# The causal convolution's output turned back to tokens on VectorE, 32x32 blocks at a time

## The reference

```
z = (u @ w_in).astype(float32)
aq, af, ai, ag, bq, bk, bv, bg, ba, bb = split(z, cuts)
o_a = _hgrn2(aq, af, ai, lb)
qkv = silu(_causal_conv(concatenate([bq, bk, bv]), conv_w))    # 4 taps, one filter for each of 3072 channels
bq, bk, bv = split(qkv, [1024, 2048])
q = l2norm(bq as 8 heads of 128) * 128 ** -0.5
k = l2norm(bk as 8 heads of 128)
o_b = _gated_delta(q, k, bv, beta, log_decay)                  # in chunks
o = concatenate([o_a gated, o_b gated])
return o @ w_out
```

## Time and profile before

| | us |
|---|---|
| time, median of 3 runs | 2742.45 |
| lowest and highest | 2741.99, 2743.88 |
| profiled execution | 2741.93 |
| its span (first to last instruction) | 2740.1 |
| PE busy in it | 2714.2 |
| DVE busy | 1684.5 |
| ACT busy | 1344.0 |

### The profile page before, as it was taken

The page is one execution under the profiler, slowest core; times in us unless marked ns, Lnnn a source line. Parts: engine busy times, 40 slices in busy tenths (PEclk is TensorE's granted clock), DMA queues, the critical chain, the costliest instruction groups (busy, mean ns, idle before and its releaser), DMA issues.

```text
span 2740.1 us, 32409 instructions
## 1 busy us (share of the span) xinstructions
PE 2714.2 (99%) x13136; PEld 2261.2 (83%) x13136; DVE 1684.5 (61%) x2280; ACT 1344.0 (49%) x1952; POOL 62.3 (2%) x85
## 2 busy tenths in 40 slices
PE   9999999999999999999999999999999999999998
PEld 7788888888888888888888888888888888887877
DVE  5666665565666666545645555666666664466666
ACT  6645444554444444434544555644444443355565
POOL 0000000000000000000100000000000000000002
PEclk9999999999999999999999999999999999999999
DMA  7764655756666666666665434666666666665444
GB/s 231 135 139 123 116 125 124 205 192 200 193 193 192 193 197 194 192 193 196 205 194 154 123 108 162 195 196 186 199 193 194 194 194 193 193 206 164 161 138 132
DMA packets 213494, 480.61 MB, mean 175 GB/s; under 512 B 15584, under 2 KB 16480, under 8 KB 212704
## 3 DMA queue, kind: packets, MB, share of 16 engines
q1 hardware_dynamic: 210848, 467.32, 59.1%
q0 software_dynamic: 2352, 11.17, 1.2%
q10 hardware_dynamic: 144, 0.05, 0.0%
HBM read 476.38 MB, written 2.10 MB: 175 GB/s over the span
## 4 chain that ended last, share of the span: by engine, by line
PE 90%; DVE 5%; ACT 2%; issue 1%; DMA 1%; POOL 0%; SPq 0%; ACTq 0%; POOLq 0%
PE PS L1116 19%; PE PS L1118 19%; PE PS L1117 19%; PE PS L1163 8%; PE PS L1164 8%; PE PS L1165 8%; DVE WL L2183 1%; DVE WORK L2350 1%; ACT WH L1657 1%; PE PS L1379 1%; PE PS L1263 1%; PE PS L1515 1%; PE PS L1282 1%; PE PS L1091 1%; DVE XL L2183 0%
## 5 line engine op out<-in xcount | busy, mean ns | idle before, releaser
L2183 DVE TENSOR_TENSOR WL<-RAW,WH 128x1024 fp32r<-128x1024 f32 x826 | 1010.5, 1225 | 817.1 <-ACT WH L1657 814.7
L1657 ACT ACTIVATE WH<-RAW 128x1024 fp32r<-128x1024 f32 x830 | 875.3, 1056 | 924.8 <-PE PS L1118 610.7
L1116 PE MATMUL PS<-WH,UTH 128*128 128x512 f32 x2396 | 951.9, 397 | 3.3 <-DVE WL L2183 1.8
L1118 PE MATMUL PS<-WH,UTL 128*128 128x512 f32 x2396 | 934.3, 390 | 0.0
L1117 PE MATMUL PS<-WL,UTH 128*128 128x512 f32 x2396 | 933.7, 390 | 0.0
L1116 PEld LDWEIGHTS PS<-WH,UTH 128*128 128x128 f32 x2396 | 450.4, 188 | 99.3 <-issue 5.2
L1118 PEld LDWEIGHTS PS<-WH,UTL 128*128 128x128 f32 x2396 | 449.9, 188 | 96.1
L1117 PEld LDWEIGHTS PS<-WL,UTH 128*128 128x128 f32 x2396 | 450.7, 188 | 88.3
L1163 PE MATMUL PS<-WH,HTH 128*128 128x512 f32 x656 | 255.2, 389 | 0.0
L1164 PE MATMUL PS<-WL,HTH 128*128 128x512 f32 x656 | 255.2, 389 | 0.0
L1165 PE MATMUL PS<-WH,HTL 128*128 128x512 f32 x656 | 255.2, 389 | 0.0
(11 more groups left out here) (420 smaller groups left out, 2211.7 us busy)
## 6 DMA issues: line engine op xcount, KB each, us to landing
RAW<-in_ffn_w_gu SPq DMA_DIRECT2D x352, 512.0 KB, 4.4
RAW<-in_ffn_w_down SPq DMA_DIRECT2D x176, 512.0 KB, 4.6
RAW<-in_ab_w_in SPq DMA_DIRECT2D x128, 512.0 KB, 4.8
RAW<-in_nsa_w_in SPq DMA_DIRECT2D x80, 512.0 KB, 3.6
RAW<-in_w_in SPq DMA_DIRECT2D x64, 512.0 KB, 4.1
RAW<-in_ab_w_out SPq DMA_DIRECT2D x32, 512.0 KB, 4.2
RAW<-in_nsa_w_out SPq DMA_DIRECT2D x32, 512.0 KB, 4.3
RAW<-in_w_out SPq DMA_DIRECT2D x16, 512.0 KB, 4.4
```

Source lines behind the costliest of these rows:

```text
L1116: e.matmul(o, lh, wh[:, j], start=k + j == 0, stop=False)
L1118: x = e.matmul(o, ll, wh[:, j], start=False, stop=k + j == NKT - 1)
L1657: e.activation(wh, raw, ACTF.Copy).then_inc(*a_hi.inc(s))
L2183: e.tensor_tensor(wl, raw, wh.bitcast(F32), ALU.subtract).then_inc(*v_lo.inc(s))
```

## The change

`cv_out` no longer uses PE or PSUM. A new step `cv_turn(hf, part, a)` has DVE transpose 32x32 blocks from `CF` straight to `Z`: for each of the four groups `a` of 32 channels it has four instructions, one for each group of 32 tokens `b` in a tile of 128, and each covers four heads and both token tiles (32 partitions x 256 elements). It reads partitions from 32a, writes from 32b. Groups 0 and 1 stand in the slot behind `cv_silu`, groups 2 and 3 in the next, then both `cv_out` together in the third. PE's `cv_out` (48 identity matmuls) and ACT's copy (12) are gone; ACT's squares stay. Waits for PE's or ACT's step now name DVE's `turn`.

```
@@ write_order, convs
                 put("cv_silu", hf, part)
-                yield from pause(2)
+                yield
+                for a in range(4):
+                    put("cv_turn", hf, part, a)
+                    if a % 2:
+                        yield
                 for t in range(2):
                     put("cv_out", hf, part, t)
-                    yield
+                yield
@@ tensor
-            @step
-            def cv_out(hf, part, t):
-                f = CF[part % 2]
-                b = take("cv_out", hf, part, t)
-                on.wait_ge(*a_cv.of("silu", hf, part))
-                for j in range(4):
-                    x = e.transpose(b[:, 128 * j:128 * j + 128], f[:, j, 128 * t:128 * t + 128], ident)
-                x.then_inc(*p_cv.inc("out", hf, part, t))
@@ scalar, cv_tap
                 if part == 2:
-                    on.wait_ge(*p_cv.of("out", hf, 0, 1))
+                    on.wait_ge(*v_cv.of("turn", hf, 0, 3))
                 elif hf:
-                    on.wait_ge(*p_cv.of("out", 0, 2 - part, 1))
+                    on.wait_ge(*v_cv.of("turn", 0, 2 - part, 3))
@@ scalar, cv_out
-                on.wait_ge(*p_cv.of("out", hf, part, t))
-                e.activation(dst, banks.ap("cv_out", hf, part, t), ACTF.Copy).then_inc(*banks.empty(a_cv, "cv_out", hf, part, t))
                 if part < 2:
-                    on.wait_ge(*a_cv.of("cv_out", hf, part, t))
+                    on.wait_ge(*v_cv.of("turn", hf, part, 3))
@@ scalar, gd_d
-                on.wait_ge(*a_cv.of("cv_out", hf, 2, i))
+                on.wait_ge(*v_cv.of("turn", hf, 2, 3))
@@ scalar, hg_a
-                    on.wait_ge(*p_cv.of("out", 1, 2, 1))
+                    on.wait_ge(*v_cv.of("turn", 1, 2, 3))
@@ vector
+            @step
+            def cv_turn(hf, part, a):
+                c = 4096 + 1024 * part + 512 * hf
+                x = CF[part % 2][32 * a:32 * a + 32].rearrange("p h (t n) -> p t h n", t=2)
+                if a == 0:
+                    on.wait_ge(*a_cv.of("silu", hf, part))
+                for b in range(4):
+                    out = Z[32 * b:32 * b + 32, :, c:c + 512].rearrange("p t (h n) -> p t h n", h=4)
+                    up = v_cv.inc("turn", hf, part, a) if b == 3 else v_cv.inc("turn", hf, part, a, b)
+                    e.transpose(out[:, :, :, 32 * a:32 * a + 32], x[:, :, :, 32 * b:32 * b + 32]).then_inc(*up)
```

## The result

| us | before | change |
|---|---|---|
| median of 6 runs each, taken side by side | 2743.36 | 2754.04 |
| lowest and highest | 2741.99, 2744.24 | 2752.06, 2754.52 |
| ratio, with its 95% interval | | 1.0038 [1.0026, 1.0051] |
| profiled execution, its span | 2741.93, 2740.1 | 2754.52, 2752.7 |
| first transpose behind the stage (L1185, now L1189) | 491.40 | 502.28 |

The change makes the kernel 0.4% slower. The interval leaves out both "no change" and the 0.2% that a measurement can tell.

What follows compares the result with a forecast made beforehand. PE, busy 99%, was taken as the bound, with DVE already what it waits for in the convolution. Span 2740.1, +10.6 (16.1 more waits, 5.5 less work), +1.3 clock, put on the median's scale: 2754 us; range 2746 to 2761.

Steps and rivals of the forecast that it cites:

- What PE is relieved of: Convolution stretch: twelve groups of four identity matmuls go, 0.46 us each, 5.5 us in all, all on the path.
- A block at 0.467: DVE's 96 transposes: each starts 0.467 us after the last, all held by changing partitions; eight take 3.73 us.
- Half 0, part 0: First convolution round: DVE's debt outruns the two-slot reserve of weight slices, so PE waits 1.6 us.
- Half 0, part 1: Second convolution round: same debt from a later start, waits of 2.2 and 0.5 us for slices, +2.0 us.
- gd_b and the bank: Delta rule one slot later: 2.2 us bank wait at the first chunk, 0.7 replacing 2.9 at the second; net 0.
- Half 1, part 0: Delta rule beside the fourth round: PE waits 3.55 us for Y, then 2.0 and 0.2; 1.9 before, +3.7 us.
- Half 1, parts 1 and 2: Last two convolution rounds: waits of 4.0 us against 1.5, +2.5; then 0.2 and 2.9 against none, +3.0.
- The clock: PE's low clock behind long waits: one fall of 1.3 us goes, two come, +1.3 net; three waits of 2.2 to 2.3 undecided.
- blocks overlap: Rival: DVE's blocks start 0.37 us apart, walk ends at +0.7 us, not slower, 2742 to 2744.5 us; 6%.
- Only the slices count: Rival: half 1's added waits of 9.2 us, for Y and its like, come at half, 2749 us; 16%.
- The clock falls more often: Rival: low clock behind all three 2.2 us waits, or blocks at 0.48 us: 2758 us each, both 2762; 20%.
- Transfers late: Rival: DVE's debt in emptying RAW buffers delays loads as well; no term in the sum, 2757 us; 3%.

Runs made afterwards that it cites:

- experiment 1: The change, but DVE turns only the last of each round's 16 blocks, PE's identity matmuls and ACT's copies still gone: 2739.44 us, 0.9988 of the kernel before.
- experiment 2: The change, but each block is written to the 32 partitions it was read from, so tokens come out misplaced: 2744.76 us, 1.0010 of the kernel before.
- experiment 3: The kernel before, nothing turned by DVE, but both cv_out of a round placed as in the change, delta rule a slot later: 1.0004 of the kernel before.
- experiment 9: The change with 12 matmuls of 512 columns put ahead of PE's 3.4 us wait for Y near 149 us: 2755.52 us, 1.0045 of the kernel before.
- experiment 4: The change in half 1 alone, eight blocks a slot; half 0 keeps PE's matmuls and ACT's copies as before: +9.7 us, 1.0036 of the kernel before.
- experiment 6: DVE turns half 1 alone, with 14 matmuls put ahead of PE's 3.88 us wait for the second chunk's Y: 2751.19 us, 1.0033 of the kernel before.

## Why the prediction held, and where its terms did not

The forecast was 2754, slower by 0.4%; it came out at 2754.04. The mechanism was right, but that the total fits to the microsecond is luck, since terms of it were off by several and cancelled.

One of its own signs went against it: "The forecast falls if [...] PE's idle time grows by less than 12 us". It grew by 10.6. The other signs of that sentence did not come (the blocks started 0.465 apart, and the 1.7 us behind the stage are waits for late loads), and the waits and their places below are those of the forecast. So I take the sign as set too tight beside a sum of 16.1 that was 4.2 too high, and not as a failure of the mechanism.

- **What PE is relieved of**: 5.5 us by the sum, 5.0 by experiment 1. "PE's busy time down by some 5 us" did not come, although the matmuls went. Busy time counts a matmul at the low clock as longer, 1.6 + 3.0 us behind two waits less the 1.3 of before. It also counts the last matmul ahead of each wait in full, 0.39 us in place of the 0.227 from start to start, and there are eight such waits more in the first 250 us, 1.3 us. Together 4.6 us come back of 5.0 to 5.5. This sign was badly chosen: busy time is no measure of work where waits are added.
- **ACT's copies at nothing**: no run isolates it, and nothing in the waits speaks against it.
- **A block at 0.467**: measured 0.465, in the way the argument had it, and experiment 2 shows the other bound, 0.35, where partitions do not change. One detail differs: not all 96 blocks are held. The first of each of the six rounds is not; that of half 0, part 0 starts at 50.28, 0.08 ahead of the end of the slice in front of it, since both read and write from partition 0.
- **Half 0, part 0**: predicted 1.6, measured 1.46. **Part 2**: 0.4 and 2.3 predicted, 0.18 and 1.95 measured.
- **Half 0, part 1**: predicted +2.0, measured +0.5 (1.15 us at the slice of 88.95, 0.66 before). The step that failed is "the same debt": it gives this round's slices the 1.22 us of a full one, and the two that follow its blocks are narrow, 0.29 us each.
- **gd_b and the bank**: 2.2 and 0.7 predicted, 2.14 and 0.56 measured; experiment 3 shows the exchange alone, at 0.8 us more of waits in all.
- **Half 1, part 0**: 3.55 for Y predicted, 3.40 measured. (The terms named there, 3.55 + 2.0 + 0.2 - 1.9, make 3.85; 3.7 went into the sum.) The 2.0 behind it is not in the trace, because PE at the low clock reached that point later than DVE did; experiment 9 brings it back, at 1.67. So this wait and the clock's loss were added up where they overlap.
- **Half 1, parts 1 and 2**: 4.0 predicted, 0.41 + 1.40 + 1.24 = 3.05 measured; and 2.9 predicted, 2.58 measured. **Behind**: 0.6 predicted; one wait of 0.42 at 374.81.
- **The sum of the waits**: 16.1 us more by the prediction. PE's idle time grew by 10.6, and with the eight overlaps of 0.16 by 11.9. Of the difference of 4.2 the part with the narrow slices is 1.5, the hidden wait 1.7 to 2.0, and the rest is spread over waits each found a little short.
- **The clock**: predicted +1.3 net, with falls of 1.3 us behind the waits of 3.55 and 2.9 and three of 2.2 undecided. There were two falls, but one was behind a wait of 2.14, one of the three, and none behind the 2.58. The term that was mis-sized is the price of one: 1.6 and 3.0 us in place of 1.3, so +3.3 net. A low stretch costs by what runs in it and by how long it lasts, and one row of before could not tell that.

In all: -5.0 + 11.9 + 3.3 = +10.2 of the 10.9 measured at the end of the stage, where the prediction had -5.5 + 16.1 + 1.3 = +11.9. By the medians the change is +10.7, 1.2 less than forecast. That 2754 was met all the same comes from the start of the sum: it stood on the median of three runs, 2742.45, and the median of the six timed beside the change is 2743.36, 0.9 higher. The chances had a slip as well: by the terms named, the part above 2748 is 0.55 + 0.20 + 0.03 + 0.11 = 0.89, not 0.86. The rivals: *blocks overlap* did not happen in the change, but experiment 2 made it happen and landed at +2.0, 2744.76, within its 2742 to 2744.5 but for the uncertainty. *Only the slices count* took the added waits of half 1 at half of 9.2, 4.6; in the change these waits are 9.2 in all (3.40 + 0.15 + 0.41 + 1.40 + 1.24 + 2.58) against 2.5 before, 6.7 more, which lies between the two, and experiment 4 loses nearly as much as the change with half 1 alone. *The clock falls more often* happened in part. *Transfers late* left no trace in the list of PE's waits.

## What to carry to other kernels

When work is moved from the bound engine to one that is half idle, do not compare shares of the span; write down what the new engine must do within one slot of the bound engine where the work is put, and who stands behind it in its queue. Eight blocks beside a slice, 5.0 us for a slot of 2.73, lost 0.4%; four at a time, in the four rounds of six that can bear them, gained 0.25%, and four at a time in all six gained nothing. Where a chain of small dependent steps shares the queue, a burst in front of each step costs its full length, while a stream with pieces made ahead only uses up its reserve.

## What the runs showed of the hardware

- **The clock falls by chance in a range of waits.** In the twelve traces PE has six waits of 2.85 to 3.88 us between 110 and 250 us, and the granted clock fell in or just behind each. Of fifteen waits between 1.95 and 2.6 us it fell behind eight, and in two executions of the same program up to that point, behind waits of 2.43 and 2.39, once not and once so. No fall followed a shorter wait there. The Trainium skill (TensorE: Matmul & The Clock Gate, section "Part 1: The HAM clock gate (the "warmup" mystery)") says that the chip's observation of activity runs free of the program, so the point at which the clock changes varies from run to run; the pair agrees.
- **A fall cost between 1.3 and 3.0 us**, least in the kernel before, where the clock was already low in the last 0.7 us of the wait (0.54 from 202.3 to 203.0), most in the change behind the wait of 3.40, where it stayed low until 155.3. Small fp32 matmuls and column matmuls both took about twice as long, 1.73 us in place of 0.81 and 0.427 in place of 0.227 from start to start, so what counts is how long PE works in the low stretch.
- **A block that starts before the last one has ended is mostly shorter too.** Experiment 2's 96 blocks, min/median/max:

```profile
L2356 DVE STREAM_TRANSPOSE BIG<-WORK x96: 390/394/442, 49.8 to 221.8; 32x256 f32<-32x256 f32 x96
```

  All of them stay in their 32 partitions, so that is not the cause: the 24 that come first in their partitions take 0.425 to 0.442 us, as in the change, and so does the block of 645.89 in the earlier trace rows, 0.43. The 72 that follow a block of the same partitions take 0.390 to 0.401 and start 0.33 to 0.37 us behind it. I had expected the distance to change and not the duration.
- **Filling a wait with matmuls holds the clock up** and gave back 2.6 us of 2.7 behind the wait in experiment 6, yet the medians show no gain, neither there beyond their uncertainty nor in experiment 9.
